# The up phases of a macaron decoder layer: the order of VectorE's low parts, and two token operands' low parts made by GpSimd

## The chip, the cores and the metric

One core of a Trainium2 chip runs the whole program. The metric is device time of one execution in microseconds (us). Engines: TensorE (PE; its weight loads are PEld), VectorE (DVE), ScalarE (ACT), GpSimd (POOL); SyncE (SP) issues the DMAs. The granted clock of TensorE is 1.0 of full speed, its level of 2.4 GHz, in all slices of the profile.

## The reference

One layer of a decoder, for 512 prompt tokens and 64 sample tokens (T = 576 in all), D_MODEL 1024, D_FF 2816, all in float32:

```
x = x + 1/2 * SwiGLU_FFN1(rmsnorm(x))
h = rmsnorm(x); P = h @ w_in            # GLU input, q_a, c_kv, k_pe, gate_a, gate_b
A = conv branch(P);  B = latent attention(P, paged cache)
x = x + w_out(sigmoid(gate_a) * A + sigmoid(gate_b) * B)
x = x + 1/2 * SwiGLU_FFN2(rmsnorm(x))

def swiglu_ffn(x, norm_g, w_gu, w_down):
    h = rmsnorm(x, norm_g)
    g, u = jnp.split(h @ w_gu, 2, axis=-1)
    return (jax.nn.silu(g) * u) @ w_down
```

The change touches the product `h @ w_gu` of the two feed-forward nets, called the up phases here.

## The kernel before, in words

Every float32 product is made of three fast ones. An operand is split into a high part (rounded by ScalarE: `xs_hi`, `w_hi`) and a low part (value minus high part, a `tensor_tensor` subtract on VectorE or GpSimd), and TensorE adds high*high, high*low and low*high.

An up phase has 22 column tiles of 128 gate and 128 up columns. The first three tiles are plain: two weight chunks each (gate, up), numbered 0 to 5 in the phase, of eight inner steps and 48 matmuls each. The other 19, the units (`seven_products`, u = 0 to 18), use a seven-product scheme on 2x2 blocks: the tokens are cut in two halves of 288, and the inner dimension in two halves. Each unit has seven products, or slots, in the order GATE1, GATE2, SUM_G, SUM_U, DIF, REST, UP2, with 12 matmuls of 128x288 each. The token operands of the seven slots (`xs`) are made once in a phase; the weight operands (`w7`, two buffers) are made anew for each unit, while TensorE works on the unit before.

VectorE's work in an up phase is a list written out by hand in `up_phase`, and each engine goes through its own list in order:

- `plain_scaled`, `plain_hidden`: the gate and up results of a plain tile times 1/rms (two instructions that read PSUM), and their product.
- `tokens_norm` (eight, 128x576) and `tokens_sum` (four, 128x1152): the normed tokens, and their sums and differences for the slots.
- `plain_low(n0, 4)` and `plain_low(n0, 5)`: low parts of plain chunks 4 and 5, for which TensorE waits on `plain_lo_done`.
- `tokens_low` (one for each slot, 128x1152): the low part of a slot's token operand. TensorE waits for it on `xs_lo` before that slot of unit 0.
- `first_seven`: the weight operands of unit 1 (`weight_sums`, `last_weight_sum`, `weight_low`, and `up2_low`, which takes the low part of the up rows' second half) between the `combine`s that add up the slots' results of unit 0. After it, `seven` does the same for the later units in a loop.

SyncE loads the raw up rows of unit u+1 into one buffer, `up_rows`, when `up2_lo` tells that `up2_low` of unit u is done. GpSimd makes the low parts of SUM_U, DIF and REST of the weights from unit 1 on (`weights_lo`); in the stretch in which the tokens' low parts are made it does nothing.

Of the kernel before, what the change touches and what calls it, by code (L numbers as in the profile page):

```python
# [14 lines left out]
F32 = mybir.dt.float32  # L15
F32R = mybir.dt.float32r
I32 = mybir.dt.int32
ALU = mybir.AluOpType
# [47 lines left out]
KH = KD // 2  # L66
GATE1, GATE2, SUM_G, SUM_U, DIF, REST, UP2 = 1, 2, 3, 4, 5, 6, 0
# [26 lines left out]
def layer(nc, x_prompt, x_sample, cache_ckv, cache_kpe, state_conv, page_table, w, const, out):  # L94

    ctx = ExitStack()
    with ctx:
# [372 lines left out]
        def split_lo(pool, n, r, size):  # L470

            pool.wait_ge(w_hi_done, n + 1)
            for c in range(4):
                part = slice(c * size // 4, (c + 1) * size // 4)
                ins = pool.tensor_tensor(w_lobuf[:, r, part], w_rawbuf[:, r, part],  # L475
                                         w_hibuf[:, r % HIS, part].bitcast(F32), ALU.subtract)
            ins.then_inc(w_lo_done, 1)
# [48 lines left out]
        def page_lo(b, t):  # L526

            return c_lo_first[:, t, :] if t < NP // 4 else c_lo[:, b, t, :]

        def pair_made(r, j):  # L530

            return r * SPLITS + (EARLY_PAIRS + 1 if j < EARLY_PAIRS else j + 3)

        def high_made(r, j):

# [57 lines left out]
        def _(sp):  # L593
# [165 lines left out]
            load_pages(1, 1)  # L759
            with sp.Fori(1, NS // 2) as i:  # L760
                for b in range(2):
                    load_pages(i * 2 + b, b, i * (2 * PAIRS) + (EARLY_PAIRS + PAIRS * (b - 2)), i * (2 * SPLITS) + (SPLITS * (b - 2) + 2))

            sp.wait_ge(lat_mm, STACKED)
            sp.dma_start(w_uv[:, :, :], w["w_uv"][0].rearrange("(k p) h d -> p k (h d)", p=P)).then_inc(late_in, 16)
# [27 lines left out]
        def _(pool):  # L793
# [25 lines left out]
            def plain_lo(f, n0, first):  # L819

                for n in range(first, 4):
                    split_lo(pool, n0 + n, (n0 + n) % RAWS, KD * P)
                pool.wait_ge(plain_lo_done, 2 * f + 2)
                pool.wait_ge(w_used, n0 + 6)
                pool.sem_inc(w_lo_done, 2)
# [620 lines left out]
        def _(pe):  # L1446
# [96 lines left out]
            def seven_products(f, u, b):  # L1543

                first = isinstance(u, int) and u == 0
                for p, slot in enumerate(IN_ORDER):
# [6 lines left out]
                    else:  # L1553
                        pe.wait_ge(w7_lo2, pool_lows(f, u, G_LOW.index(slot) + 1))
                    if first:
                        pe.wait_ge(xs_lo, 7 * f + p + 1)
                        if p in (0, 4):
                            pe.wait_ge(unit_read, (q_ffn1_up, q_ffn2_up)[f] + 2 * PLAIN[f] - (0 if p else 2))
                    elif slot == GATE1:
                        pe.wait_ge(part_read, unit_sums(f, u, 1, 0))  # L1560
                    else:
                        pe.wait_ge(c_done, unit_sums(f, u, 7, (-6, -5, -4, -2, -1, 0)[p - 1]))
# [470 lines left out]
        def _(dve):  # L2033
# [185 lines left out]
            def first_seven(f):  # L2219

                weight_sums(f, 1, 1)
                weight_low(f, 1, 1, GATE1)
                up2_low(f, 1, 1)
                combine(f, 0, GATE2)
                last_weight_sum(f, 1, 1)
                weight_low(f, 1, 1, GATE2)
                combine(f, 0, SUM_G)
                weight_low(f, 1, 1, SUM_G)
                combine(f, 0, SUM_U)
                combine(f, 0, DIF)  # L2230
                combine(f, 0, REST)
# [12 lines left out]
            def up_phase(f, v, n0, q0, gain):  # L2244
                dve.wait_ge(rstd_done, v + 1)
                plain_scaled(f, n0, q0, 0)
                for k in range(KH):
                    tokens_norm(f, gain, k)
                plain_hidden(f, q0, 0)
                plain_low(n0, 4)  # L2250
                for k in range(KH, KD):
                    tokens_norm(f, gain, k)
                tokens_sum(f, 0)
                tokens_sum(f, 1)
                plain_low(n0, 5)
                tokens_sum(f, 2)
                tokens_sum(f, 3)
                plain(f, n0, q0, 1)
                for slot in IN_ORDER[:4]:
                    tokens_low(f, slot)  # L2260
                plain_scaled(f, n0, q0, 2)
                for slot in IN_ORDER[4:6]:
                    tokens_low(f, slot)
                plain_hidden(f, q0, 2)
                tokens_low(f, UP2)
                first_seven(f)
                with dve.Fori(0, (SEVEN[f] - 3) // 2) as i:
                    seven(f, (i, 1), 1, (i, 2), (i, 0))
# [608 lines left out]
```

## Time and profile before

| | |
|---|---|
| time, median of 3 runs | 1545.67 us (1543.26, 1545.67, 1550.80) |
| profiled execution | 1546.08 us, of which the span of the trace is 1544.3 us |
| PE busy | 1524.7 us (99%) |
| DVE / ACT / POOL busy | 1036.5 / 660.2 / 662.3 us |
| first up phase | begins at 15 us with the first weights; unit 0 at 63.25 us |
| second up phase | unit 0 at 1180.69 us |

The span is the time from the program's first to its last recorded instruction; the time of the execution is 1.78 us more. Times below are counted from the span's start. A timeline row gives start, duration, engine, line, operation, output and inputs, shapes and count; what stands in brackets is the idle time of the engine before it, and who ended it.

### The profile page before, as it was taken

Reading aid. Unit: us, or ns where it says so; the run is one execution under the profiler, and the core shown is the slowest. Engines: PE = TensorE matmul, PEld = TensorE weight load, DVE = VectorE, ACT = ScalarE, POOL = GpSimd, SP = SyncE. Lnnn points to the kernel's source line nnn. Section 1 sums busy time; section 2 is a strip of 40 time slices with the busy share of each in tenths; the row PEclk is TensorE's granted clock in tenths of the full one; section 3 lists DMA queues with packets and bytes.
Section 4 is the critical chain, followed back from the end, with each engine's and each line's share of the span. In section 5 each row is a group of like instructions: output and inputs, shape, how many; then the busy total and the mean of one; then the engine's idle time right before and its main releaser. Section 6 shows DMA issues by size and latency. Waiting matters only on the chain.

```text
span 1544.3 us, 32007 instructions
## 1 busy us (share of the span) xinstructions
PE 1524.7 (99%) x11171; PEld 1473.4 (95%) x11171; DVE 1036.5 (67%) x1672; ACT 660.2 (43%) x1258; POOL 662.3 (43%) x680
## 2 busy tenths in 40 slices
PE   8999999999999999999999999999999999999998
PEld 8999999999999999588999999988999999999998
DVE  4998888611259976865877777864669988884101
ACT  5453444522221242364666666652434444453110
POOL 3165455544445654320233333223552645564342
PEclk9999999999999999999999999999999999999999
DMA  6133233322233332001322222312222323242222
GB/s 175 42 104 100 84 105 96 91 84 75 83 85 99 88 110 61 0 1 51 85 63 62 65 63 62 88 56 82 83 81 64 103 83 105 84 129 57 76 85 71
DMA packets 231678, 122.82 MB, mean 80 GB/s; under 512 B 28415, under 2 KB 228327, under 8 KB 231572
## 3 DMA queue, kind: packets, MB, share of 16 engines
q1 hardware_dynamic: 230510, 120.83, 27.9%
q8 instruction: 55, 0.90, 0.2%
q10 hardware_dynamic: 1070, 0.74, 0.2%
q14 instruction: 43, 0.35, 0.1%
HBM read 118.31 MB, written 3.58 MB: 79 GB/s over the span
## 4 chain that ended last, share of the span: by engine, by line
PE 90%; DVE 4%; ACT 2%; issue 2%; DMA 1%; POOL 0%; SPq 0%; DVEq 0%; ACTq 0%; POOLq 0%
PE ps L489 40%; PE ps L1566 27%; PE ps L1956 11%; PE ps L1848 1%; PE ps L1719 1%; PE ps L1773 1%; PE ps L1748 1%; PE ps L1887 1%; PE ps L1866 1%; PE ps L1916 1%; PE ps L1867 1%; DMA x_nat<-in_x_sample 1%; PE ps L1763 1%; PE ps L1725 1%; ACT sq L1358 0%
## 5 line engine op out<-in xcount | busy, mean ns | idle before, releaser
L475 POOL TENSOR_TENSOR w_lobuf<-w_rawbuf,w_hibuf 128x256 fp32r<-128x256 f32 (+1 forms) x332 | 314.0, 977 | 367.5 <-ACT w_hibuf L468 367.4
L1566 PE MATMUL ps<-xs,w 128*128 128x288 f32 x3192 | 427.4, 296 | 2.2 <-DVE w L2082 2.2
L1566 PEld LDWEIGHTS ps<-xs,w 128*128 128x128 f32 x3192 | 426.8, 188 | 2.6 <-issue 2.6
L815 POOL TENSOR_TENSOR w<-w_raw,w 128x256 fp32r<-128x256 f32 x216 | 222.3, 1062 | 223.2 <-DVE w_raw L2070 143.3
L468 ACT ACTIVATE w_hibuf<-w_rawbuf 128x1024 fp32r<-128x1024 f32 (+1 forms) x89 | 104.4, 1173 | 350.9 <-PE ps L489 345.5
L489 PE MATMUL ps<-a_hi,w_hibuf 128*128 128x288 f32 x704 | 152.5, 297 | 0.0
L489 PE MATMUL ps<-a_hi,w_lobuf 128*128 128x288 f32 x704 | 152.2, 297 | 0.0
L489 PE MATMUL ps<-a_lo,w_hibuf 128*128 128x288 f32 x704 | 150.1, 294 | 0.0
L489 PE MATMUL ps<-x_hi,w_hibuf 128*128 128x288 f32 x656 | 142.8, 299 | 2.9 <-POOL w_lobuf L805 0.8
L489 PE MATMUL ps<-x_lo,w_hibuf 128*128 128x288 f32 x656 | 141.0, 296 | 0.0
L489 PE MATMUL ps<-x_hi,w_lobuf 128*128 128x288 f32 x656 | 141.0, 296 | 0.0
L1024 ACT ACTIVATE w<-w_raw 128x512 fp32r<-128x512 f32 x228 | 128.9, 622 | 5.4 <-DVE w_raw L2076 3.3
L1956 PE MATMUL ps<-kq_hi,cT_hi 128*128 128x288 f32 x512 | 117.8, 311 | 1.3 <-ACT sq L1358 0.8
L2293 DVE SCALAR_TENSOR_TENSOR xT<-ps,xT 128x576 f32<-128x576 f32 x23 | 17.4, 757 | 148.8 <-PE ps L489 148.8
L489 PEld LDWEIGHTS ps<-a_hi,w_hibuf 128*128 128x128 f32 x704 | 113.7, 189 | 0.0
L489 PEld LDWEIGHTS ps<-a_lo,w_hibuf 128*128 128x128 f32 x704 | 112.8, 188 | 0.0
L489 PEld LDWEIGHTS ps<-a_hi,w_lobuf 128*128 128x128 f32 x704 | 112.5, 188 | 0.0
L489 PEld LDWEIGHTS ps<-x_hi,w_hibuf 128*128 128x128 f32 x656 | 105.8, 189 | 4.4 <-issue 2.4
L2082 DVE TENSOR_TENSOR w<-w_raw,w 128x512 fp32r<-128x512 f32 x120 | 109.4, 917 | 0.1
L1956 PE MATMUL ps<-kq_hi,cT_lo 128*128 128x288 f32 x512 | 109.4, 295 | 0.0
L2322 DVE SCALAR_TENSOR_TENSOR y<-ext,cols,y 128x512 f32<-128x512 f32 x120 | 106.6, 889 | 4.1 <-DVE y L2322 1.4
L1956 PE MATMUL ps<-kq_lo,cT_hi 128*128 128x288 f32 x512 | 109.4, 295 | 0.0
(361 smaller groups left out, 2766.7 us busy)
## 6 DMA issues: line engine op xcount, KB each, us to landing
w_raw<-in_ffn_w_gu SPq DMA_DIRECT2D x76, 256.0 KB, 2.9
up_rows<-in_ffn_w_gu SPq DMA_DIRECT2D x74, 256.0 KB, 3.2
c_nat<-in_cache_ckv SPq DMA_DIRECT2D x128, 128.0 KB, 2.0
w_rawbuf<-in_w_in SPq DMA_DIRECT2D x58, 256.0 KB, 3.2
w_rawbuf<-in_ffn_w_down SPq DMA_DIRECT2D x32, 384.0 KB, 4.1
w_rawbuf<-in_ffn_w_down SPq DMA_DIRECT2D x32, 320.0 KB, 3.4
w_rawbuf<-in_ffn_w_gu SPq DMA_DIRECT2D x24, 256.0 KB, 3.4
w_rawbuf<-in_w_out SPq DMA_DIRECT2D x16, 256.0 KB, 3.2
```

The costliest lines, as they stand in the source:

```text
L468: act.activation(w_hibuf[:, r % HIS, 0:size], w_rawbuf[:, r, 0:size], ACT.Copy).then_inc(w_hi_done, 1)
L475: ins = pool.tensor_tensor(w_lobuf[:, r, part], w_rawbuf[:, r, part], w_hibuf[:, r % HIS, part].bitcast(F32), ALU.subtract)
L489: mm = pe.matmul(ps[0:width, 2 * s + h, 0:HALF], a, b[:, k, h * HALF:(h + 1) * HALF], start=first and i == 0 and j == 0, stop=last and i = ...
L815: ins = pool.tensor_tensor(w7[b][:, slot, 1, part], w7_raw[b][:, slot, 1, part], w7[b][:, slot, 0, part].bitcast(F32), ALU.subtract)
L1024: act.activation(w7[b][:, slot, 0, :], src, ACT.Copy).then_inc(w7_hi, 1)
L1566: mm = pe.matmul(ps[:, seven_bank(f, slot), 0:HALF], m, xs[:, slot, n, k, :], start=k == 0 and j == 0, stop=k == KH - 1 and j == 2)
L1719: mm = pe.matmul(ps[0:n, 2 * s + b, 0:QL], qaT[k][:, i * P:i * P + n], w_uq[:, k, b * QL:(b + 1) * QL], start=k == 0, stop=k == QL // P - 1)
L1725: mm = pe.matmul(ps[0:n, 2 * s, :], cT[:, k, i * P:i * P + n], w_uk[:, k, :], start=k == 0, stop=k == 1)
L1956: mm = pe.matmul(ps[:, page_banks(t) + half, 0:KQ], a, m[:, half, cols], start=k == 0 and j == 0, stop=k == 1 and j == 2)
L2082: dve.tensor_tensor(w7[b][:, slot, 1, :], w7_raw[b][:, slot, 1, :], w7[b][:, slot, 0, :].bitcast(F32), ALU.subtract).then_inc(w7_lo, 1)
L2293: dve.scalar_tensor_tensor(x2, unit(s), scale, x2, op0=ALU.mult, op1=ALU.add).then_inc(x_done, 1)
L2322: dve.scalar_tensor_tensor(dst, src, cw, dst, op0=ALU.mult, op1=ALU.add).then_inc(conv_p_step, 1)
```

## The change

In `up_phase` of VectorE, `plain_low(n0, 4)` moves ahead of the last two of the first four `tokens_norm` and of `plain_hidden(0)`; `plain_low(n0, 5)` moves ahead of the second `tokens_sum`; the `tokens_low` of REST and UP2 are taken out. GpSimd makes these two at the end of `plain_lo`, one instruction each, and TensorE waits for them on `split_made`, whose counts elsewhere are shifted by two for each phase. In `first_seven`, `up2_low` of unit 1 moves behind `weight_low` of SUM_G. All of it happens in both up phases.

```diff
+        TOKEN_SPLITS = 2
@@ gpsimd, plain_lo
                 for n in range(first, 4):
                     split_lo(pool, n0 + n, (n0 + n) % RAWS, KD * P)
+                for blk, made in ((REST, 3), (UP2, 7)):
+                    pool.wait_ge(xs_sum, 4 * f + 4)
+                    pool.wait_ge(xs_hi, 7 * f + made)
+                    pool.tensor_tensor(xs[:, blk, 1], xs_raw[:, blk, 1], xs[:, blk, 0].bitcast(F32), ALU.subtract).then_inc(split_made, 1)
                 pool.wait_ge(plain_lo_done, 2 * f + 2)
@@ tensor, seven_products
                     if first:
-                        pe.wait_ge(xs_lo, 7 * f + p + 1)
+                        if slot in (REST, UP2):
+                            pe.wait_ge(split_made, f * (TOKEN_SPLITS + STACKED * SPLITS) + (1 if slot == REST else 2))
+                        else:
+                            pe.wait_ge(xs_lo, 5 * f + p + 1)
@@ vector, first_seven
                 weight_low(f, 1, 1, GATE1)
-                up2_low(f, 1, 1)
                 combine(f, 0, GATE2)
...
                 weight_low(f, 1, 1, SUM_G)
+                up2_low(f, 1, 1)
                 combine(f, 0, SUM_U)
@@ vector, up_phase
                 plain_scaled(f, n0, q0, 0)
-                for k in range(KH):
+                tokens_norm(f, gain, 0)
+                tokens_norm(f, gain, 1)
+                plain_low(n0, 4)
+                for k in range(2, KH):
                     tokens_norm(f, gain, k)
                 plain_hidden(f, q0, 0)
-                plain_low(n0, 4)
                 for k in range(KH, KD):
                     tokens_norm(f, gain, k)
                 tokens_sum(f, 0)
+                plain_low(n0, 5)
                 tokens_sum(f, 1)
-                plain_low(n0, 5)
...
                 plain_scaled(f, n0, q0, 2)
-                for slot in IN_ORDER[4:6]:
-                    tokens_low(f, slot)
+                tokens_low(f, IN_ORDER[4])
                 plain_hidden(f, q0, 2)
-                tokens_low(f, UP2)
                 first_seven(f)
```

VectorE's list in the first up phase, from the first `plain_scaled` to the last `tokens_sum`, before (`xs_raw<-xT` are `tokens_norm`, `xs_raw<-xs_raw` are `tokens_sum`, `w_lobuf` is `plain_low`, `a<-tb,ta` is `plain_hidden`):

```order
L2124 TENSOR_TENSOR tb<-ps,rstd 128x576 [waits w_used]
L2153 SCALAR_TENSOR_TENSOR xs_raw<-xT,cols,rstd 128x2x288 x4
L2140 TENSOR_TENSOR a<-tb,ta 128x576 [waits silu_done,unit_read]
L2242 TENSOR_TENSOR w_lobuf<-w_rawbuf,w_hibuf 128x1024 [waits w_hi_done]
L2153 SCALAR_TENSOR_TENSOR xs_raw<-xT,cols,rstd 128x2x288 x4
L2162 TENSOR_TENSOR xs_raw<-xs_raw 128x1152 [waits xs_norm]
L2162 TENSOR_TENSOR xs_raw<-xs_raw 128x1152 [waits xs_sum,xs_norm]
L2242 TENSOR_TENSOR w_lobuf<-w_rawbuf,w_hibuf 128x1024 [waits w_hi_done]
L2162 TENSOR_TENSOR xs_raw<-xs_raw 128x1152 [waits xs_sum,xs_norm] x2
```

The same place in the changed kernel:

```order
L2133 TENSOR_TENSOR tb<-ps,rstd 128x576 [waits w_used]
L2162 SCALAR_TENSOR_TENSOR xs_raw<-xT,cols,rstd 128x2x288 x2
L2251 TENSOR_TENSOR w_lobuf<-w_rawbuf,w_hibuf 128x1024 [waits w_hi_done]
L2162 SCALAR_TENSOR_TENSOR xs_raw<-xT,cols,rstd 128x2x288 x2
L2149 TENSOR_TENSOR a<-tb,ta 128x576 [waits silu_done,unit_read]
L2162 SCALAR_TENSOR_TENSOR xs_raw<-xT,cols,rstd 128x2x288 x4
L2171 TENSOR_TENSOR xs_raw<-xs_raw 128x1152 [waits xs_norm]
L2251 TENSOR_TENSOR w_lobuf<-w_rawbuf,w_hibuf 128x1024 [waits w_hi_done]
L2171 TENSOR_TENSOR xs_raw<-xs_raw 128x1152 [waits xs_sum,xs_norm] x3
```

Both `w_lobuf` instructions have come forward, the first past two `tokens_norm` and the `plain_hidden`, the second past one `tokens_sum`.

GpSimd's list from the low parts of plain chunk 3 of the first phase to the loop over the units (L829 is that loop; L815 is `weights_lo`), before:

```order
L475 TENSOR_TENSOR w_lobuf<-w_rawbuf,w_hibuf 128x256 [waits w_hi_done]
L475 TENSOR_TENSOR w_lobuf<-w_rawbuf,w_hibuf 128x256 x3
L829 UNCONDITIONAL_BRANCH [waits plain_lo_done,w_used]
L829 ISA
L813 ISA [waits w7_sum]
L815 TENSOR_TENSOR w_1_73<-w_raw_75,w_1_73 128x256 [waits w7_hi]
```

The same place in the changed kernel:

```order
L475 TENSOR_TENSOR w_lobuf<-w_rawbuf,w_hibuf 128x256 [waits w_hi_done]
L475 TENSOR_TENSOR w_lobuf<-w_rawbuf,w_hibuf 128x256 x3
L828 TENSOR_TENSOR xs<-xs_raw,xs 128x1152 [waits xs_hi,xs_sum] x2
L835 UNCONDITIONAL_BRANCH [waits plain_lo_done,w_used]
L835 ISA
L815 ISA [waits w7_sum]
```

The two token operands stand between the last plain chunk and the loop.

## Rows read from the trace of the kernel before

**Rows 1.** Busy time, share of the span and count of each engine

```profile
PE 1524.7 (99%) x11171; PEld 1473.4 (95%) x11171; DVE 1036.5 (67%) x1672; ACT 660.2 (43%) x1258; POOL 662.3 (43%) x680
```

**Rows 2.** Waits of PE: us in total, times, longest

```profile
PE ps L1566 <- DVE w L2082: 2.2, 2, 1.6
```

**Rows 3.** Timeline of PE, first up phase

```profile
49.84 0.53 PE L489 MATMUL ps<-x_hi,w_hibuf 128*128 128x288 f32 x2 [0.55 <-DVE w_lobuf L2242]
...
56.75 0.53 PE L489 MATMUL ps<-x_hi,w_hibuf 128*128 128x288 f32 x2 [0.25 <-DVE w_lobuf L2242]
...
63.25 11.36 PE L1566 MATMUL ps<-xs,w 128*128 128x288 f32 x84
75.23 1.86 PE L1566 MATMUL ps<-xs,w 128*128 128x288 f32 x12 [0.62 <-DVE w L2082]
78.65 46.58 PE L1566 MATMUL ps<-xs,w 128*128 128x288 f32 x347 [1.55 <-DVE w L2082]
```

**Rows 4.** Timeline of PE, second up phase

```profile
1180.69 24.48 PE L1566 MATMUL ps<-xs,w 128*128 128x288 f32 x182
```

**Rows 5.** Timeline of DVE, first up phase

```profile
44.99 3.00 DVE L2153 SCALAR_TENSOR_TENSOR xs_raw<-xT,cols,rstd 128x576 f32<-128x576 f32 x4
...
48.58 1.22 DVE L2242 TENSOR_TENSOR w_lobuf<-w_rawbuf,w_hibuf 128x1024 fp32r<-128x1024 f32 x1
...
56.62 2.82 DVE L2162 TENSOR_TENSOR xs_raw<-xs_raw 128x1152 f32<-128x1152 f32 x2
...
60.92 0.76 DVE L2140 TENSOR_TENSOR a<-tb,ta 128x576 f32<-128x576 f32 x1 [0.16 <-ACT ta L1000]
61.60 5.16 DVE L2168 TENSOR_TENSOR xs<-xs_raw,xs 128x1152 fp32r<-128x1152 f32 x4
66.67 0.76 DVE L2124 TENSOR_TENSOR ta<-ps,rstd 128x576 f32<-128x576 f32 x1
...
68.00 2.62 DVE L2168 TENSOR_TENSOR xs<-xs_raw,xs 128x1152 fp32r<-128x1152 f32 x2
...
82.87 0.69 DVE L2066 TENSOR_TENSOR w_raw<-up_rows 128x512 f32<-128x512 f32 x1
...
86.93 0.86 DVE L2082 TENSOR_TENSOR w<-w_raw,w 128x512 fp32r<-128x512 f32 x1
...
92.69 0.69 DVE L2066 TENSOR_TENSOR w_raw<-up_rows 128x512 f32<-128x512 f32 x1
```

**Rows 6.** Timeline of ACT, first up phase

```profile
60.72 2.21 ACT L1007 ACTIVATE xs<-xs_raw 128x1152 fp32r<-128x1152 f32 x2
```

**Rows 7.** Timeline of DVE, second up phase

```profile
1162.84 1.23 DVE L2242 TENSOR_TENSOR w_lobuf<-w_rawbuf,w_hibuf 128x1024 fp32r<-128x1024 f32 x1 [1.22 <-ACT w_hibuf L468]
...
1170.89 2.82 DVE L2162 TENSOR_TENSOR xs_raw<-xs_raw 128x1152 f32<-128x1152 f32 x2
...
1175.88 5.16 DVE L2168 TENSOR_TENSOR xs<-xs_raw,xs 128x1152 fp32r<-128x1152 f32 x4
...
1197.60 0.68 DVE L2066 TENSOR_TENSOR w_raw<-up_rows 128x512 f32<-128x512 f32 x1
```

**Rows 8.** Groups of POOL by line and shape: count, busy us, mean ns

```profile
L886 POOL TENSOR_TENSOR q_nat<-q_nat,gqk 128x768 f32<-128x768 f32 x4 | 7.3, 1820 | 14.6 <-ACT sq L1230 14.6
L805 POOL TENSOR_TENSOR w_lobuf<-w_rawbuf,w_hibuf 128x256 fp32r<-128x256 f32 x8 | 5.6, 737 | 21.7 <-ACT w_hibuf L468 21.7
```

**Rows 9.** Timelines of DVE and POOL where both subtract from SBUF

```profile
35.65 5.13 POOL L475 TENSOR_TENSOR w_lobuf<-w_rawbuf,w_hibuf 128x256 fp32r<-128x256 f32 x4 [3.57 <-ACT w_hibuf L468]
...
37.81 1.22 DVE L2088 TENSOR_TENSOR w<-up_rows,w 128x512 fp32r<-128x512 f32 x1
...
289.53 2.76 DVE L2236 TENSOR_TENSOR a_lo<-a,a_hi 128x576 fp32r<-128x576 f32 x4
...
289.78 3.32 POOL L475 TENSOR_TENSOR w_lobuf<-w_rawbuf,w_hibuf 128x352 fp32r<-128x352 f32 x1 [10.70 <-ACT w_hibuf L468]
```

**Rows 10.** The tile up_rows, from 60 to 110 us: its DMAs' landing

```profile
DMA to landing us min/median/max: 2.9/3.3/4.9
```

More of the change, by code:

```diff
@@ L528, in page_lo @@
             return c_lo_first[:, t, :] if t < NP // 4 else c_lo[:, b, t, :]
+        TOKEN_SPLITS = 2
         def pair_made(r, j):
-            return r * SPLITS + (EARLY_PAIRS + 1 if j < EARLY_PAIRS else j + 3)
+            return r * SPLITS + TOKEN_SPLITS + (EARLY_PAIRS + 1 if j < EARLY_PAIRS else j + 3)
         def high_made(r, j):
@@ L761, in _ @@
                 for b in range(2):
-                    load_pages(i * 2 + b, b, i * (2 * PAIRS) + (EARLY_PAIRS + PAIRS * (b - 2)), i * (2 * SPLITS) + (SPLITS * (b - 2) + 2))
+                    load_pages(i * 2 + b, b, i * (2 * PAIRS) + (EARLY_PAIRS + PAIRS * (b - 2)), i * (2 * SPLITS) + (SPLITS * (b - 2) + 2 + TOKEN_SPLITS))
             sp.wait_ge(lat_mm, STACKED)
```

## The prediction

> **What bounds the kernel now.** I read the busy line first: TensorE is busy for 1524.7 us, 99% of the span [rows 1], so no more than some twenty us of idle time are left in the whole program, most of it at the start and the end. Then the list of TensorE's waits: among them 2.2 us for VectorE's low parts of weights, in two waits [rows 2]. Then TensorE's timeline in both up phases. In the first it waits four times: 0.55 us before plain chunk 4, 0.25 us before chunk 5, 0.62 us before unit 1, 1.55 us before the second slot of unit 1; together 2.97 us [rows 3]. In the second it runs through: unit 0 begins at 1180.69 us with 182 matmuls and no bracket [rows 4]. So the change can win some 3 us in the first phase and nothing in the second, 0.2% of the time.
>
> In the steady part a matmul takes 46.58 / 347 = 0.134 us [rows 3]; a slot of 12 is 1.61 us, a unit of 84 is 11.27 us. VectorE's list for a unit takes 92.69 - 82.87 = 9.82 us while it is behind [rows 5]: it catches up 1.4 us in each unit, so what the up phase's beginning costs is settled within the first units and doesn't repeat in the loop.
>
> As a mark for the first phase I take TensorE's start of unit 1 without gaps: its second slot began at 78.65, less 1.61, is 77.04 us. Unit 2 then wants to begin at 77.04 + 11.27 = 88.31, and its first low part was done at 86.93 + 0.86 = 87.79 [rows 3, 5]: only 0.5 us of slack. That matters below.
>
> **The change part by part, first phase.**
>
> *The two plain low parts.* A `tokens_norm` takes 0.74 us (3.00 for four), a `plain_low` 1.2, a sum 1.41 (2.82 for two) [rows 5]. Two norms from 44.99 on, then `plain_low` 4: done at 47.7 instead of 49.8. `plain_low` 5 comes one sum, 1.41 us, earlier. Both waits of chunks 4 and 5, 0.80 us, go, and TensorE is ready for unit 0 at 63.25 - 0.80 = 62.45. The list up to the last sum has the same instructions and still ends at 56.62 + 2.82 = 59.44. What is late next is the low part of GATE1: it ended at 61.60 + 1.29 = 62.9, so at best 0.35 of the 0.80 us is kept.
>
> *REST and UP2 on GpSimd.* VectorE loses two of 1.29 us (5.16 for four), 2.6 us in each phase [rows 5]. The trace has no GpSimd subtract of 1152 columns. From 256 columns at 737 ns and 768 at 1820 ns [rows 8] it is 2.115 ns a column, so 1820 + 384 x 2.115 = 2630 ns as an estimate. Two of them are 5.3 us, and TensorE needs them last of all, five and six slots after unit 0 began: their own duration is hidden.
>
> *What they do to VectorE.* When both engines subtract from SBUF, one holds the other up. Four GpSimd subtracts took 5.13 us, 1.28 each instead of 0.74, and VectorE's of 512 columns took 1.22 beside them, 0.69 without [rows 5, 9]: they take turns. But when VectorE already runs without a gap, GpSimd waits until the run is over: its subtract came at 289.78, during the first of four VectorE subtracts, and took 3.32 us, ending only after them at 292.29 [rows 9].
>
> REST's operands are ready at 59.44. VectorE then reads PSUM (`plain_scaled`), so GpSimd starts and holds on to 62.1. The `plain_hidden` of 60.92 reads two SBUF tiles and waits 1.2 us for it [rows 5]. GATE1's low part is done at 64.1, and TensorE starts unit 0 there, 0.85 later than before. UP2's high part is made at 60.72 + 2.21 = 62.93 [rows 6], in the middle of VectorE's run of four low parts. I take the nearest row, that of 289.78: GpSimd waits to the run's end at 61.60 + 5.16 + 1.2 = 67.9 and runs to 70.5. VectorE's two PSUM reads (66.67 to 68.00 before, 1.33 us [rows 5]) pass meanwhile; DIF's low part then waits, and is done at 71.8. TensorE wanted it at 64.1 + 4 x 1.61 = 70.5. Three slots later, at 76.6, unit 0 is over: 0.4 earlier than the mark of 77.04. The bounds of this step: no hold at all, unit 0 over at 74.2 (62.9 + 11.27, 2.8 gained); or UP2 goes between the first two low parts, and VectorE is 1.3 us later at DIF: over at 78.0 (1.0 lost).
>
> The Trainium skill ("SBUF — State Buffer", Who interferes with whom) has a VectorE instruction with two SBUF inputs and a GpSimd one that reads SBUF exclude each other, the first to issue holding the port for its whole instruction. By the letter UP2 would come right after the one that runs, which is the later bound; the row at 289.78, where three more VectorE instructions went first, speaks for the other.
>
> *`up2_low` of unit 1, moved behind three low parts.* It is needed only in the last slot of unit 1. But SyncE loads the `up_rows` of unit 2 after it: a stretch from DIF's low part, with `plain_hidden` 0.7, four weight sums 2.6, four low parts 3.6 (two beside GpSimd) and two `combine`s 0.8, is 7.7 us, so it ends at 79.5. The second DMA is issued 0.5 later, and lands 3.3 us after that [rows 10], at 83.3. The weight sums of unit 2 began at 82.87 [rows 5] and now wait 0.4; the first low part of unit 2 comes at 88.2, TensorE wants it at 76.6 + 11.27 = 87.9. So unit 2 begins at 88.2 instead of 88.3: of the 0.4 us, 0.1 is left. First phase: -0.1 us.
>
> **Second phase.** Here `plain_low` 4 waits for ScalarE until 1162.84, after 1.22 us of idle time [rows 7], and now two norms and the `plain_hidden`, 2.15 us, stand behind that wait instead of ahead of it. The last sum ends at 1170.89 + 2.82 + 2.15 = 1175.86 instead of 1173.71. REST holds the port to 1178.5; the `plain_hidden` ends at 1179.2, GATE1's low part at 1180.45, in time for 1180.69 [rows 4]. The run of four ends at 1184.3; UP2 runs to 1186.9, DIF's low part to 1188.1. TensorE wants it at 1180.69 + 4 x 1.61 = 1187.1 and waits 1.0. With UP2 between the low parts, GATE2 would be 2 us late and DIF 0.3 more: 2.2 in all; without any hold, nothing. `up2_low` ends at 1195.8, `up_rows` land at 1199.6, 2.0 after the weight sums of unit 2 began before (1197.60 [rows 7]); the low part of unit 2 comes at 1204.5, TensorE is there at 1192.9 + 11.27 = 1204.2: another 0.3. Second phase: +1.2 us, rounded.
>
> **Sum.** -0.1 + 1.2 = +1.1 us on the profiled execution's 1546.08 (span 1544.3 and 1.78 around it), that is 1547.2. The median of the three runs shown is 0.4 lower; from there 1545.67 + 1.1 = **1546.8 us**: no change that can be measured. The three runs lie 7.5 us apart, and 0.5% (7.7 us) is about what a measurement of this kernel can tell from no change.
>
> **Rivals.**
>
> *GpSimd costs VectorE nothing.* Then VectorE is 2.6 us lighter and both late waits of the first phase go: -2.8 us there, and 0 in the second, where nothing waited: 1542.9. For it: REST meets PSUM reads for half of its time. Against: the 1.22 us beside GpSimd [rows 9]. Chance 0.15.
>
> *GpSimd goes between the low parts.* First phase: unit 0 over at 78.0 and unit 2's low part no earlier: +1.0; second: +2.2. Slower by 3.2: 1548.9. For it: the turns of the row at 35.65 [rows 9]. Against: 289.78. Chance 0.25.
>
> *The late `up_rows` decide (the slower side).* If they land after 4.9 us [rows 10], and the low parts are held as in the rival above, they land at 86.3 and 1202.4, 3.4 and 4.8 us after the weight sums began before. Unit 2's low part is then 1.9 us late in each phase: 1.0 + 1.9 + 2.2 + 1.9 = +7.0, 1552.7. It decides from a landing of about 3.5 us on. For it: the load stands in a chain with 0.5 us of slack. Against: 3.3 is the median. Chance 0.06.
>
> *The change removes no wait.* If chunk 4's weights in the first phase come from ScalarE no sooner than now, `plain_low` 4 gains nothing, and the forecast is 0.1 worse: 1546.9. Chance 0.04, with nothing else changed.
>
> **How the numbers follow.** The forecast has 0.5, the rivals 0.15, 0.25, 0.06 and 0.04. The range reaches from the first rival, less 1 us, to the second, plus 2 us for the spread of the runs: 1541.8 to 1551.0. Faster by over 0.5% (under 1537.9) can't come out of a gain bounded by 3 us, only out of the runs' spread: 0.03. Slower by over 0.5% (above 1553.4) needs the third rival and more: 0.05. Within 0.5%: 0.92.
>
> **What would show it.** In the changed kernel's first phase: no wait before chunks 4 and 5; a new wait of 1 to 2 us before unit 0, and one of about 1.3 us before its slot DIF; no wait inside unit 1. In the second: a wait of about 1 us within unit 0, where there was none. GpSimd's REST about 2.6 us long, its UP2 over 6 us long as recorded, most of it waiting; `plain_hidden` at 60.9 us 2 us long. Wrong would be: low parts of 1.29 us with GpSimd's beside them (the first rival), a low part of over 3.5 us in the run of four (the second), or a wait of 2 us at the start of unit 2 (the third).

## The result, and the profile after

The changed kernel's median is 1552.52 us (15 runs, 1551.76 to 1554.41), that of the kernel before 1546.97 in the same comparison: a ratio of 1.0040 [1.0031, 1.0048]. It is slower by 5.6 us by the medians. One of the 15 runs of the kernel before took 3820.17 us, and the ratio leaves it out. The forecast was 1546.8 us, no change, and the range, to 1551.0, doesn't hold the time.

The profiled execution took 1551.76 us, with a span of 1549.8, which is 5.5 more than before. The busy line of the changed kernel:

```profile
PE 1529.6 (99%) x11171; PEld 1478.7 (95%) x11171; DVE 1039.9 (67%) x1668; ACT 660.0 (43%) x1258; POOL 670.3 (43%) x684
```

TensorE has the same 11171 matmuls as in [rows 1] and is busy 4.9 us longer; an engine that only waits longer shows no more busy time, so some matmuls have become slower, which is a first hint at the clock (a third of the 4.9 us lies near 716 us, between the phases, and isn't the change's, as the last experiment shows). VectorE has four instructions fewer and 3.4 us more of busy time: what it no longer does, it spends in longer instructions.

TensorE's two longest groups of waits in the changed kernel (engine, line, what it waited for: us in total, times, longest):

```profile
PE ps L1575 <- DVE xs L2177: 3.9, 2, 2.0
PE ps L1575 <- issue: 2.1, 1, 2.1
```

They stand in unit 0 of the two up phases: the low parts of token operands. The waits for low parts of weights [rows 2] and the two before plain chunks [rows 3] are gone. TensorE's timeline from unit 0 on, first and second phase, in two fences:

```profile
62.39 1.82 PE L1575 MATMUL ps<-xs,w 128*128 128x288 f32 x12 [2.13 <-issue]
66.16 64.04 PE L1575 MATMUL ps<-xs,w 128*128 128x288 f32 x466 [1.95 <-DVE xs L2177]
```

```profile
1182.53 1.76 PE L1575 MATMUL ps<-xs,w 128*128 128x288 f32 x12
1186.22 43.99 PE L1575 MATMUL ps<-xs,w 128*128 128x288 f32 x316 [1.93 <-DVE xs L2177]
```

In the first phase TensorE waits for GATE1's low part (the profile names no releaser there and writes "issue", but that low part is done at 62.29 us and TensorE begins at 62.39), does its slot of 12, waits again for GATE2's, and then runs through the rest of the units shown, 64 us, without a bracket; before, the brackets stood at unit 1 [rows 3]. In the second phase, which had none [rows 4], the wait for GATE2 is new.

VectorE's timeline of the changed kernel in the first phase answers to [rows 5] (the instructions of the run of four one by one):

```profile
59.13 1.89 DVE L2149 TENSOR_TENSOR a<-tb,ta 128x576 f32<-128x576 f32 x1 [0.16 <-ACT ta L1006]
...
60.95 1.34 DVE L2177 TENSOR_TENSOR xs<-xs_raw,xs 128x1152 fp32r<-128x1152 f32 x1
...
62.21 3.80 DVE L2177 TENSOR_TENSOR xs<-xs_raw,xs 128x1152 fp32r<-128x1152 f32 x1
...
65.94 1.35 DVE L2177 TENSOR_TENSOR xs<-xs_raw,xs 128x1152 fp32r<-128x1152 f32 x1
```

And GpSimd's two new instructions in it:

```profile
57.72 2.68 POOL L828 TENSOR_TENSOR xs<-xs_raw,xs 128x1152 fp32r<-128x1152 f32 x1 [18.73 <-DVE xs_raw L2171]
61.28 3.52 POOL L828 TENSOR_TENSOR xs<-xs_raw,xs 128x1152 fp32r<-128x1152 f32 x1 [0.87 <-ACT xs L1013]
```

REST runs from 57.72 to 60.40, and the `plain_hidden` that began at 59.13 ends only after it: 1.89 us instead of 0.76. UP2 is recorded from 61.28, while GATE1's low part runs (to 62.29), until 64.80. From 62.29 on that is 2.5 us, nearly a whole subtract: it got the next turn. GATE2's low part, recorded from 62.21, is done only at 66.01, after 3.80 us instead of 1.34. TensorE begins its second slot at 66.16. The second phase reads the same (GpSimd at 1181.32 us for 3.54).

In the second phase VectorE is also later as a whole. Its wait for ScalarE's high part, 1.22 us before [rows 7], is the place:

```profile
1164.68 1.23 DVE L2251 TENSOR_TENSOR w_lobuf<-w_rawbuf,w_hibuf 128x1024 fp32r<-128x1024 f32 x1 [4.86 <-ACT w_hibuf L468]
...
1173.40 4.28 DVE L2171 TENSOR_TENSOR xs_raw<-xs_raw 128x1152 f32<-128x1152 f32 x3
```

VectorE stands idle for 4.86 us, and two norms and the `plain_hidden` are behind that wait.

The clock, in the stretches behind the new waits (columns: stretch in us, its length, busy us and count of PE, PEld, DVE, ACT and POOL, granted clock, DMA share, GB/s):

```profile
67.40:70.80 3.40, 3.40 (x16) 3.40 (x15) 3.40 (x4) 1.55 (x3) 0.00 (x0) 0.50 0.24 67
...
1186.90:1190.30 3.40, 3.40 (x16) 3.40 (x15) 3.40 (x5) 0.99 (x2) 0.00 (x0) 0.50 0.47 128
```

A granted clock of 0.50 is 1.2 GHz. In 3.4 us TensorE does 16 matmuls, where it did 28 in the kernel before at the start of unit 0 in the second phase:

```profile
1180.70:1184.10 3.40, 3.40 (x28) 3.40 (x27) 3.40 (x5) 0.69 (x1) 0.00 (x0) 1.00 0.57 163
```

That is an estimated 12 x 0.134 = 1.6 us lost in each phase. The opening says that the granted clock is 1.0 in all slices of the profile. The profile's page prints a 9 for every slice, which means 90% or more of 38.6 us, so a short stretch at half clock doesn't show there. The kernel before has two in its trace:

```profile
18.00:21.40 3.40, 3.40 (x19) 3.38 (x18) 1.51 (x3) 1.69 (x5) 0.00 (x0) 0.50 0.53 154
...
717.70:721.10 3.40, 3.40 (x15) 3.07 (x16) 2.41 (x7) 1.99 (x4) 0.00 (x0) 0.50 0.11 16
```

One like the first, near the program's start, is in every trace here (it begins between 10.8 and 20.5 us); the second lies between the phases. Behind the start no such stretch lay in an up phase.

**Where the 5.5 us come from.** I put the same matmul, by its number among the 11171, of both traces side by side and read how much later it starts. From the 150th (26.95 us before) to the 1001st (144.46) the changed kernel falls back by 2.10 us; from the 8472nd (1179.62) to the 9001st (1250.33) by 3.68. In the first phase: the chunk waits gone -1.2, GATE1 +2.2, GATE2 +2.2, clock +1.6, unit 1's two waits gone -2.6. In the second: GATE2 +2.1, clock +1.6. (A wait costs up to 0.2 us more than its bracket.) The two phases together make 5.8; the program's start and the stretch between the phases, which differ from one execution of a kernel to the next by 1 to 2 us, make -0.3.

### The profile page after: what moved, and what is told of

It is laid out like the page before. It is cut to its first block, busy times and chain, and to the rows that moved or that the text cites. A ratio compares the mean times of both kernels' runs of the same rounds, so it can differ in the third digit from the quotient of the medians.

```text
span 1549.8 us, 32007 instructions
## 1 busy us (share of the span) xinstructions
PE 1529.6 (99%) x11171; PEld 1478.7 (95%) x11171; DVE 1039.9 (67%) x1668; ACT 660.0 (43%) x1258; POOL 670.3 (43%) x684
## 4 chain that ended last, share of the span: by engine, by line
PE 88%; DVE 5%; issue 2%; ACT 2%; DMA 1%; SPq 0%; POOL 0%; DVEq 0%; ACTq 0%; POOLq 0%
PE ps L489 38%; PE ps L1575 28%; PE ps L1965 10%; PE ps L1857 1%; PE ps L1728 1%; PE ps L1782 1%; PE ps L1757 1%; PE ps L1896 1%; PE ps L1875 1%; PE ps L1925 1%; PE ps L1876 1%; DVE xs_raw L2162 1%; DMA x_nat<-in_x_sample 1%; PE ps L1772 1%; PE ps L1734 1%
## 5 line engine op out<-in xcount | busy, mean ns | idle before, releaser
L817 POOL TENSOR_TENSOR w<-w_raw,w 128x256 fp32r<-128x256 f32 x216 | 219.1, 1047 | 184.4 <-DVE w_raw L2079 148.9
L1042 ACT ACTIVATE ta<-ta 128x576 f32<-128x576 f32 x38 | 26.1, 686 | 197.7 <-DVE ta L2199 197.7
```

Of the source, the lines that this page charges most:

```text
L817: ins = pool.tensor_tensor(w7[b][:, slot, 1, part], w7_raw[b][:, slot, 1, part], w7[b][:, slot, 0, part].bitcast(F32), ALU.subtract)
L1042: act.activation(ta[:, :], ta[:, :], ACT.Silu).then_inc(gate_act, 1)
```

## The experiments

Each part of the change alone, then one suspected cost at a time. The table shows the ratio to the kernel before, and how far a profiled execution fell back over each phase, measured as above.

```
what is changed                        ratio  [95%]             1st    2nd phase
all (the changed kernel)               1.0040 [1.0031, 1.0048]  +2.10  +3.68
lists and up2_low, no GpSimd           1.0019 [1.0010, 1.0028]  +0.68  +2.34
GpSimd alone                           1.0013 [1.0000, 1.0026]  +1.07  +0.58
all, waits filled with matmuls         1.0042 [1.0029, 1.0055]  +1.67  +3.26
all, UP2 after the run of four         1.0027 [1.0018, 1.0037]  +0.71  +2.23
up2_low alone                          1.0008 [0.9999, 1.0017]  +0.61  +0.70
plain_low order alone                  1.0015 [1.0006, 1.0024]  +0.31  +1.69
zeros by GpSimd, up2_low at its place  0.9987 [0.9978, 0.9996]  -2.44   0.00
mended order, first phase alone        1.0001 [0.9992, 1.0010]  -0.41  +0.31
all, UP2 after GATE1's low part        one execution               +1.71  +3.24
REST zeros, UP2 subtracted             one execution               +0.54  +2.14
the changed kernel again               one execution               +2.48  +3.67
the kernel before again                one execution               +0.21   0.00
```

**The lists and `up2_low`, without GpSimd.** The changed VectorE order in the kernel before, all seven token operands by VectorE.

```diff
+                tokens_norm(f, gain, 0)
+                tokens_norm(f, gain, 1)
+                plain_low(n0, 4)
...
                 tokens_sum(f, 0)
+                plain_low(n0, 5)
                 tokens_sum(f, 1)
-                plain_low(n0, 5)
...
                 weight_low(f, 1, 1, GATE1)
-                up2_low(f, 1, 1)
...
                 weight_low(f, 1, 1, SUM_G)
+                up2_low(f, 1, 1)
```

> The kernel before with the new order of VectorE's list and the later up2_low, but REST's and UP2's low parts still on VectorE. Theory (GpSimd's two subtracts hold VectorE's port, TensorE then waits some 2 us at unit 0, and its granted clock falls for a stretch behind that wait): without GpSimd no such wait, chunks 4 and 5 of the first phase no longer wait, 1 to 2 us faster than before, ratio 0.999; no half-clock stretch near unit 0 in either phase. Rival (the order itself costs: in the second phase 2.15 us of VectorE's work stands behind a wait for ScalarE, and up_rows come late): 3 to 5 us slower than before, ratio 1.002 to 1.003.

It is slower by 0.19%, as the rival had it and not the theory. TensorE's waits from unit 1 on, in both phases (but for 0.30 us at 1194.94; before unit 0 it waits 1.08 for GATE1):

```profile
74.14 1.87 PE L1566 MATMUL ps<-xs,w 128*128 128x288 f32 x12 [0.69 <-DVE w L2082]
76.42 9.94 PE L1566 MATMUL ps<-xs,w 128*128 128x288 f32 x72 [0.41 <-DVE w L2082]
87.72 37.53 PE L1566 MATMUL ps<-xs,w 128*128 128x288 f32 x279 [1.37 <-DVE w L2082]
...
1206.40 23.78 PE L1566 MATMUL ps<-xs,w 128*128 128x288 f32 x176 [1.61 <-DVE w L2082]
```

A wait at unit 2 has taken the place of the 1.55 us in unit 1 [rows 3]. Its reason is on VectorE, in the first weight sum of unit 2:

```profile
82.68 0.69 DVE L2066 TENSOR_TENSOR w_raw<-up_rows 128x512 f32<-128x512 f32 x1 [0.81 <-DMA up_rows<-in_ffn_w_gu]
```

VectorE stands waiting for `up_rows`. SyncE issues that load at 78.74 us here, at 76.40 before and at 79.10 in the changed kernel: it goes where `up2_low` goes. The mechanism of the third rival is there without GpSimd.

**GpSimd alone.** The changed kernel with VectorE's plain order and `up2_low` of before.

```diff
+                for blk, made in ((REST, 3), (UP2, 7)):
...
+                    pool.tensor_tensor(xs[:, blk, 1], xs_raw[:, blk, 1], xs[:, blk, 0].bitcast(F32), ALU.subtract).then_inc(split_made, 1)
...
-                for slot in IN_ORDER[4:6]:
-                    tokens_low(f, slot)
+                tokens_low(f, IN_ORDER[4])
                 plain_hidden(f, q0, 2)
-                tokens_low(f, UP2)
```

> The kernel before with only REST's and UP2's low parts on GpSimd; VectorE's list otherwise in its old order. Theory: first phase UP2's subtract goes between GATE1's and GATE2's low parts, TensorE waits about 0.9 us before unit 0 and 2 us before its second slot; second phase VectorE is 2.15 us earlier than in the changed kernel, so GATE2's low part is done at about 1182.1 where TensorE wants it at 1182.3, and hardly waits. About 2 us slower in all if the clock stays, 3.5 if it falls behind the wait of the first phase: ratio 1.001 to 1.002. Rival (GpSimd's work alone costs all): ratio 1.004, with a wait of 2 us in the second phase too.

```profile
65.06 1.81 PE L1575 MATMUL ps<-xs,w 128*128 128x288 f32 x12 [0.76 <-issue]
68.83 56.46 PE L1575 MATMUL ps<-xs,w 128*128 128x288 f32 x417 [1.96 <-DVE xs L2177]
```

GATE2's wait is there with the old lists, and all later brackets of the first phase are gone. So in the first phase the wait is GpSimd's doing alone. In the second TensorE doesn't wait here, as the theory had it: there GpSimd's hold (3.82 us) costs only where VectorE is late as well. In this trace the clock stayed at 1.00 behind the wait. By the ratio, whose interval begins at 1.0000, this part alone is barely told from no change.

**The waits filled.** The changed kernel, in which TensorE runs throwaway matmuls into the free half of the slot's own bank before each of the three slots that wait. The 8 of the edit stand in the trace as 16 matmuls of 128x128 each time.

```diff
+                        if p == 0:
+                            pe.wait_ge(unit_read, (q_ffn1_up, q_ffn2_up)[f] + 2 * PLAIN[f] - 2)
+                        if p == 1 or (p == 0 and f == 0):
+                            keep_busy(8, ps[:, seven_bank(f, slot), HALF:HALF + P])
```

> The changed kernel, where TensorE does 8 throwaway 128x128 matmuls (about 1.7 us) into the free half of the slot's own bank before it waits for GATE1 and GATE2 of unit 0 in the first phase, and for GATE2 in the second. They add nothing that is used. Theory (the clock falls because TensorE stood still): the waits are as long as before, but the granted clock stays at 1.0 behind them, and 2 x 1.6 us come back: ratio about 1.002 against before. Rival (the half-clock stretch comes at that place anyway, or by chance): the stretch stays, ratio 1.004 or a little more.

The granted clock stayed at 1.00 in both phases (columns as above, first phase), and the time did not move: 1552.60. The theory was right on the clock and wrong on the time.

```profile
65.00:75.00 10.00, 9.79 (x75) 9.39 (x74) 10.00 (x10) 3.37 (x7) 1.45 (x1) 1.00 0.39 107
```

```profile
67.72 21.47 PE L1579 MATMUL ps<-xs,w 128*128 128x288 f32 x156
89.71 35.51 PE L1579 MATMUL ps<-xs,w 128*128 128x288 f32 x264 [0.51 <-DVE w L2095]
```

Of the 1.6 us of the clock, most is paid in other places: TensorE falls back by 0.3 us at slot DIF of unit 0 and by 0.7 at unit 2, where it is now too early for the late `up_rows`. By the table 0.4 us is gained in each phase. The fall of the clock is a cost that stands in front of others of nearly its size. The timed runs fit that. Eight of the 15 runs of the changed kernel have a mean granted clock of 0.994, as the profiled one, and six have 0.996; the medians of the two groups are 1552.3 and 1553.9 us, so the higher clock was no faster; where their stretches at 0.50 lie isn't on record.

**UP2 after the run of four.** GpSimd waits for VectorE's fourth low part: what the forecast had assumed of the chip, now forced.

```diff
+                    if blk == UP2:
+                        pool.wait_ge(xs_lo, 5 * f + 4)
```

> The changed kernel, where GpSimd begins UP2's low part only after VectorE's run of four low parts. Theory: GATE2's low part is no longer held, the waits of about 2 us before slot GATE2 go in both phases; instead DIF's low part is held, a wait of about 1.3 us at slot DIF in the first phase and 1.0 in the second, as the prediction had it; if the clock stays behind these shorter waits, 1 us slower than before, ratio 1.0005; if it falls all the same, 1.003. Rival (it doesn't matter between which low parts UP2 stands): ratio 1.004.

TensorE, then GpSimd's UP2, then VectorE:

```profile
66.00 6.62 PE L1577 MATMUL ps<-xs,w 128*128 128x288 f32 x48 [2.08 <-issue]
73.88 16.30 PE L1577 MATMUL ps<-xs,w 128*128 128x288 f32 x120 [1.26 <-issue]
```

```profile
69.88 2.69 POOL L830 TENSOR_TENSOR xs<-xs_raw,xs 128x1152 fp32r<-128x1152 f32 x1 [5.86 <-DVE xs L2179]
```

```profile
64.56 5.15 DVE L2179 TENSOR_TENSOR xs<-xs_raw,xs 128x1152 fp32r<-128x1152 f32 x4
...
70.96 2.82 DVE L2179 TENSOR_TENSOR xs<-xs_raw,xs 128x1152 fp32r<-128x1152 f32 x1
```

With the assumption made true, the chain in unit 0 comes out as forecast: four low parts in 5.15 us, DIF's held for 2.82, TensorE's wait for it 1.26 us (1.23 in the second phase) against 1.3 and 1.0 in the forecast. The clock stayed at 1.00 in both phases. The kernel is some 2 us better than the changed one (0.13% by the ratios). But it is still slower than before by 0.27%, where the theory expected 0.05% if the clock stays. Its trace falls back by 0.71 + 2.23 = 2.9 us, where the prediction's sum had 1.1. The rest is mostly at unit 2 (brackets of 0.59 and 0.49 us) and in the second phase's wait at DIF, which costs 1.4 us.

**The two halves of the order.** First `up2_low` alone:

```diff
                 weight_low(f, 1, 1, GATE1)
-                up2_low(f, 1, 1)
                 combine(f, 0, GATE2)
...
                 weight_low(f, 1, 1, SUM_G)
+                up2_low(f, 1, 1)
```

> The kernel before with one edit: up2_low of unit 1 behind the low part of SUM_G, in both phases. In e1_order TensorE waited 1.37 and 1.61 us at the start of unit 2, where up_rows had landed late. Theory (the late load costs only where VectorE is late as well, through the new order of its list): first phase the second slot of unit 1 gains about 1.1 us and unit 2 gives it back through up_rows; second phase up_rows land about when they are wanted; in all 0 to 0.8 us slower, ratio 1.0000 to 1.0005. Rival (the load alone makes all of e1_order's 3 us): ratio 1.002, waits of over 1.3 us at unit 2 in both phases.

1548.09 us, a ratio that isn't clear of no change; the trace shows the mechanism. The wait at unit 2 is 1.25 us in the first phase, and 0.43 in the second, where there was none:

```profile
88.44 36.73 PE L1566 MATMUL ps<-xs,w 128*128 128x288 f32 x273 [1.25 <-DVE w L2082]
...
1205.51 24.72 PE L1566 MATMUL ps<-xs,w 128*128 128x288 f32 x183 [0.43 <-DVE w L2082]
```

Then the order of the two `plain_low` alone:

```diff
-                for k in range(KH):
+                tokens_norm(f, gain, 0)
+                tokens_norm(f, gain, 1)
+                plain_low(n0, 4)
+                for k in range(2, KH):
                     tokens_norm(f, gain, k)
                 plain_hidden(f, q0, 0)
-                plain_low(n0, 4)
...
                 tokens_sum(f, 0)
+                plain_low(n0, 5)
                 tokens_sum(f, 1)
-                plain_low(n0, 5)
```

> The kernel before with one edit: the two plain_low earlier in VectorE's list, in both phases; up2_low, REST and UP2 as before. Theory (the list behind the last sum ends when it did, so the waits of chunks 4 and 5 only move to unit 0 and unit 1; in the second phase VectorE is 2.15 us late): first phase 0 against before, second phase TensorE waits about 1 us in all at unit 1; ratio 1.0005 to 1.001. Rival (the order alone makes e1_order's loss): ratio 1.002.

1548.79 us, between the theory's time and the rival's. In the first phase the chunk waits go and nothing is won: TensorE waits 1.10 us for GATE1 in their place, and the two waits in unit 1 stay (0.70 and 1.56). In the second, VectorE's wait for ScalarE is again 4.86 us, and TensorE pays at unit 1:

```profile
1193.94 36.26 PE L1566 MATMUL ps<-xs,w 128*128 128x288 f32 x269 [1.43 <-DVE w L2082]
```

**Zeros instead of the subtract.** GpSimd writes REST's and UP2's low parts without reading anything; `up2_low` at its old place. The low parts of these two operands are left out of the result.

```diff
-                    pool.tensor_tensor(xs[:, blk, 1], xs_raw[:, blk, 1], xs[:, blk, 0].bitcast(F32), ALU.subtract)
+                    pool.memset(xs[:, blk, 1].bitcast(F32), 0.0)
```

> The changed kernel with up2_low in its old place, and GpSimd writing zeros into REST's and UP2's low parts instead of the subtract: it reads nothing of SBUF, and REST's and UP2's low parts of the tokens are left out. Theory (the two subtracts cost because their reads keep VectorE's two-input instructions from starting): plain_hidden takes 0.76 us, the run of four low parts 5.16 us, GATE1's low part is in time to within 0.5 us; first phase about 2.5 us faster than before, second 0; ratio 0.9985. Rival (VectorE is late for another reason, its list or GpSimd's mere presence): ratio 1.003.

The fastest of all, 1544.61 us, though with these low parts left out. VectorE, GpSimd's UP2, and TensorE:

```profile
62.91 5.16 DVE L2177 TENSOR_TENSOR xs<-xs_raw,xs 128x1152 fp32r<-128x1152 f32 x4
```

```profile
64.36 1.06 POOL L828 MEMSET xs<- 128x1152 f32 x1 [2.49 <-ACT xs L1013]
```

```profile
64.37 60.81 PE L1575 MATMUL ps<-xs,w 128*128 128x288 f32 x451 [0.96 <-issue]
```

GpSimd works in the middle of VectorE's run, and the run takes 5.16 us as alone [rows 5]. No wait is left in either phase but GATE1's. This is what the change, without the move of `up2_low`, would have been worth had GpSimd's reads cost VectorE nothing: 1.9 us by the medians.

**A mended order.** VectorE's new order in the first phase alone, `up2_low` only one low part later, no GpSimd.

```diff
+                if not f:
+                    tokens_norm(f, gain, 0)
+                    tokens_norm(f, gain, 1)
+                    plain_low(n0, 4)
...
                 weight_low(f, 1, 1, GATE1)
-                up2_low(f, 1, 1)
                 combine(f, 0, GATE2)
                 weight_low(f, 1, 1, GATE2)
+                up2_low(f, 1, 1)
```

> A version meant to keep what is good in the change: no subtracts on GpSimd; the two plain_low earlier in the first phase only, as the second waits for ScalarE there; up2_low of unit 1 right behind the low part of GATE2, so that up_rows is loaded about 1 us later than before and not 3. Theory: first phase the second slot of unit 1 gains about 1 us, unit 2 starts without a wait over 0.5 us, second phase as before; ratio 0.9994. Rival (the load is late already so, or the gain is given back at the start of unit 2): ratio 1.000 to 1.001.

1547.16 us, no different from before, as the rival had it. The first phase loses 0.96 us before unit 0 and 0.69, 0.41 and 0.41 in unit 1, 2.5 in all against 2.97: VectorE as a whole is late, and an order moves the wait about.

**Who goes next.** The changed kernel, with GpSimd asking for UP2 only once GATE1's low part is done, when GATE2's is already running.

```diff
+                    if blk == UP2:
+                        pool.wait_ge(xs_lo, 5 * f + 1)
```

> The changed kernel, where GpSimd asks for UP2's operands only once GATE1's low part is done, so early in GATE2's. Theory (GpSimd goes next, right behind the instruction that runs): the third low part, SUM_G, is held and takes some 3.8 us, the second doesn't; GpSimd's record is about 3.6 us long. Rival (only the first instruction behind one that was itself held lets GpSimd in; later the run keeps the port): GpSimd waits to the end of the run, its record is over 6 us long, and none of the four is held.

VectorE's third low part, GpSimd's UP2 and TensorE:

```profile
64.75 3.82 DVE L2179 TENSOR_TENSOR xs<-xs_raw,xs 128x1152 fp32r<-128x1152 f32 x1
```

```profile
63.72 3.62 POOL L830 TENSOR_TENSOR xs<-xs_raw,xs 128x1152 fp32r<-128x1152 f32 x1 [2.05 <-DVE xs L2179]
```

```profile
68.71 3.43 PE L1577 MATMUL ps<-xs,w 128*128 128x288 f32 x24 [1.62 <-DVE xs L2179]
```

Now the third low part is held, and TensorE waits a slot later, for SUM_G: in this run of four, GpSimd goes right behind the low part that runs when it asks.

**A run that wasn't held before.** REST's low part by zeros (left out), UP2's subtracted: if the run at 289.78 [rows 9] kept GpSimd out because VectorE came to it without having been held, this one should too.

```diff
+                    if blk == REST:
+                        pool.memset(xs[:, blk, 1].bitcast(F32), 0.0)
```

> The changed kernel, where GpSimd writes zeros for REST (REST's low part of the tokens is left out) and subtracts only UP2: plain_hidden is then not held, and the run of four low parts comes without a gap behind it. Theory (GpSimd goes next, right behind the instruction that runs): one low part takes some 3.8 us, GpSimd's record is about 3.6 us long. Rival (a run that began without being held keeps the port, as at 289.78 us of the kernel before): the run takes 5.16 us and GpSimd's record is over 5 us long.

```profile
62.12 0.76 DVE L2152 TENSOR_TENSOR a<-tb,ta 128x576 f32<-128x576 f32 x1 [0.16 <-ACT ta L1009]
62.80 7.64 DVE L2180 TENSOR_TENSOR xs<-xs_raw,xs 128x1152 fp32r<-128x1152 f32 x4
```

```profile
64.27 3.68 POOL L831 TENSOR_TENSOR xs<-xs_raw,xs 128x1152 fp32r<-128x1152 f32 x1 [2.51 <-ACT xs L1016]
```

The `plain_hidden` is free, 0.76 us, and the run is held all the same, 7.64 us. GpSimd asks here during the second low part, and the third takes 3.83 us. So having been held before isn't the reason.

**Both kernels again.** Do the stretches at 0.50 belong to the change, or to one execution?

> The changed kernel once more, for its clock. Theory (the fall behind the waits at unit 0 comes with them, but not each time, as e2_gpsimd waited 1.96 us and kept its clock): the waits of about 2 us are there again in both phases; half-clock stretches near them in at least one phase. Rival (the falls of the first profile were chance): none.

> The kernel before once more, for its clock. Theory (the half-clock stretch near 716 us, 3.4 or 6.8 us long, differs from run to run of the same program): 3.4 or 6.8 us, and 1.5 us between them from 715 to 733 us; no half-clock stretch near unit 0 of either phase. Rival (it belongs to the changed kernel): 3.4 us.

The changed kernel showed them in both phases again, 6.8 and 3.4 us long (TensorE's GATE1 slot of this execution first):

```profile
65.13 2.14 PE L1575 MATMUL ps<-xs,w 128*128 128x288 f32 x12 [2.08 <-issue]
```

```profile
66.40:73.20 6.80, 5.16 (x23) 4.84 (x22) 6.80 (x6) 1.20 (x3) 1.15 (x1) 0.50 0.37 104
...
1189.40:1192.80 3.40, 3.40 (x17) 3.40 (x16) 3.40 (x4) 1.81 (x4) 0.00 (x0) 0.50 0.50 141
```

The first of them begins within GATE1's slot, behind the wait of 2.08 us alone and ahead of GATE2's of 1.64, and the clock is at 0.50 through the second wait. The kernel before again had none in an up phase but the one at its start. Near 716 us, between the phases, both kernels have one, of 3.4 us in some executions and 6.8 in others; that difference isn't the change's.

## Why the prediction was wrong, step by step

**The two plain low parts.** Right. Both chunk waits are gone. "What is late next is the low part of GATE1" is what the order alone shows (1.10 us); in the changed kernel, with REST's hold, that wait is 2.13 (forecast 64.1 - 62.45 = 1.65), since TensorE is ready 1.2 us earlier and not 0.8. Unit 0 begins 0.97 us later than before, where the forecast had 0.85.

**REST and UP2 on GpSimd.** The estimate of 2630 ns from two smaller shapes [rows 8] met 2.68 us.

**What they do to VectorE: the step that failed.** REST's half was right: `plain_hidden` was held for 1.1 us (forecast 1.2), and GATE1's low part was done 4.65 us after the last sum (4.66). For UP2 I took "the nearest row, that of 289.78: GpSimd waits to the run's end". It didn't wait; it went next, and GATE2's low part took 3.80 us. That was the sign named for the second rival, "a low part of over 3.5 us in the run of four". With UP2 forced to the run's end the forecast's waits in unit 0 appeared nearly as sized, and the trace fell back by 2.9 us and not 5.8. So of the 4.7 us by which the trace misses the sum's +1.1, about 2.9 belong to this step, with the clock's fall behind it. The other 1.8 are there still with UP2 placed later, most of it in terms that the sum had too small: the wait at unit 2 (0.7 us in each phase, forecast 0.3), the second phase's wait at DIF (1.4, forecast 1.0), and some 0.3 less gained in unit 1.

The Trainium skill ("SBUF — State Buffer", Who interferes with whom) says that the order of issue decides which of the two engines blocks. The trace agrees here, with GpSimd's subtract of 61.28 us ahead of the low part recorded from 62.21; at 289.78 three further VectorE subtracts went first. I let one row outweigh the rule, and that row had another shape (576 columns, not 1152) and another place. Nearer was the row at 35.65 [rows 9], where the engines took turns; it was in the text as the rival's evidence. The width alone isn't the reason. The same trace has a VectorE addition of 576 columns that stood next in line and was held, 1.75 us instead of 0.83 for the same line at 918.3 us, by a GpSimd that had stood idle before, as at 289.78:

```profile
911.87 3.40 POOL L923 TENSOR_TENSOR c_lo_first<-c_nat,c_hi 128x512 fp32r<-128x512 f32 x2 [11.73 <-ACT c_hi L1332]
...
912.45 1.75 DVE L2672 TENSOR_TENSOR ln_acc<-ln_acc,y 128x576 f32<-128x576 f32 x1
```

The same happens at 953.07 us. Counted over that trace, where GpSimd began a two-input instruction while one of VectorE's with two SBUF inputs ran and another stood next in line, GpSimd went ahead of that one at least 14 times, and let it by three times (at 35.65 for one instruction, at 289.78 and at 1404.54). The forecast rested on the rarer order.

**The second rival's price.** Its mechanism was the right one, and its +3.2 us was too small. The waits themselves came out near (without the clock's 1.6, first phase +0.5 against +1.0, second +2.1 against +2.2); what it left out is what follows the waits. In the changed kernel that is TensorE's clock, 1.6 us in each phase by its first trace. The filled waits show that this isn't simply added: with the clock held, the waits at DIF and at unit 2 take all but 0.4 of it.

**The third rival.** Its time, 1552.7 us, is nearest to the measured 1552.5, but by luck. Its sign, a wait of about 2 us at the start of unit 2, isn't in the changed kernel's trace in either phase, and what it adds to the second rival (1.9 us from `up_rows` in each phase) isn't what the trace shows.

**`up2_low`.** The mechanism was right: the load moves with it. The size was not, where VectorE runs without GpSimd: 1.25 us of wait at unit 2 for `up2_low` alone in the first phase and 0.43 in the second, against 0.3 in each in the forecast. In the changed kernel TensorE shows none of it, since it comes later to unit 2; VectorE waits there for `up_rows` all the same:

```profile
83.07 0.69 DVE L2075 TENSOR_TENSOR w_raw<-up_rows 128x512 f32<-128x512 f32 x1 [0.84 <-DMA up_rows<-in_ffn_w_gu]
```

It costs again where one of the other losses is taken away: 0.5 to 0.6 us at unit 2 with the waits filled, and with UP2 placed later.

**Second phase.** VectorE's 2.15 us behind ScalarE was right as a mechanism. Its price in the order alone, +1.7 us at unit 1, was hidden in the forecast's sum behind the later waits.

**The sum.** The first phase fell back by 2.10 us where the forecast had -0.1, the second by 3.68 where it had +1.2. The parts alone fell back by 1.65 (GpSimd), 2.0 (lists) and 1.3 us (`up2_low`) over both phases, 5.0 together; the whole fell back by 5.8. No part gained. GpSimd took two instructions of 1.29 us from VectorE in each phase and gave 1.13 + 2.46 us of holding back: more than it took. The range ended 2 us above the second rival's time, for the runs' spread alone; it had no room for what follows a wait.

**What stays open.** Why three VectorE subtracts went ahead of GpSimd at 289.78 in the kernel before. It isn't chance: the same subtract takes 3.32 to 3.37 us at this place and at its twin in the second feed-forward net (1404.54) in all 14 traces, old lists and new. Having been held earlier isn't the reason, and the rows at 912.45 and 953.07 speak against the width of 576 columns; the spacing of the instructions and the kinds of operands weren't tried apart. Nor is it shown what tells the waits that the clock fell behind from those of the same length that it didn't.

## What to carry to other kernels

A two-input subtract moved from VectorE to GpSimd frees VectorE only if VectorE has no instruction with two SBUF inputs to do while it runs. Otherwise, as here, VectorE stands still for what is left of GpSimd's subtract (1.13 and 2.46 us), and what matters is whose instruction is next at that moment. An instruction that releases a buffer carries the load behind it along, so its lateness is paid a unit later, and one that is put ahead of a wait in one use of a shared function can come to stand behind a wait in the other use. Where two rows of a trace disagree on who goes first, price the forecast by both and let the range hold the worse one with its follow-ups.

## What the runs showed of the hardware that was not expected

- GpSimd's subtract from SBUF went right behind the VectorE subtract that was running, ahead of VectorE's low parts already in line, in all traces in which it asked during their run (the second low part was held when it asked during the first, the third when it asked during the second: 3.80 to 3.83 us instead of 1.34). At 289.78 us of the kernel before it didn't. A GpSimd write without reads, 1.06 us, didn't hold VectorE: the run took 5.16 us.
- In both traces of the changed kernel and in both phases, TensorE ran for 0.7 to 1.5 us behind a wait of 1.93 to 2.08 us, and then the granted clock was 0.50 for 3.4 or 6.8 us. Waits of 1.96 us (behind one of 0.76), of 2.08 (with 1.26 later) and of 2.10 (with 1.62 later) were not followed by that, in one trace each.
